# Eight vector-by-matrix units of a modulation moved to VectorE, three operations a step, with their buffer refilled by halves

## The reference

```python
def hybrid_layer(x, ...):
    ...
    h = rms_norm(x, g_ffn_pre)
    gate, up = jnp.split(jnp.matmul(h, w_gate_up), [FFN_HIDDEN], axis=-1)
    f = jnp.matmul(jax.nn.silu(gate) * up, w_down)
    return x + rms_norm(f, g_ffn_post)

# second block
mod_l = jnp.split((jax.nn.silu(c) @ w_ada[i] + b_ada[i])[:, None, :], 6, axis=-1)
mod_c = jnp.split((jax.nn.silu(c_ctx) @ w_ada[i] + b_ada[i])[None, None, :], 6, axis=-1)
hc = modulate(xc, mod_c[0], mod_c[1])
hl = modulate(xl, mod_l[0], mod_l[1])
```

## Time and profile before

| | us |
|---|---|
| median of three runs | 1605.41 |
| the three runs | 1602.16, 1605.41, 1607.61 |
| the profiled execution's own time | 1604.94 |
| its span, first to last instruction | 1603.1 |
| PE busy in the span | 1555.9 |
| feed-forward blocks 2 to 21 of layer 0 | 150.3 to 275 |
| the same of layer 1 | 486.5 to 615 |

### The profile page before, as it was taken

One profiled execution on the slowest core, in us unless ns is written; L12 is line 12 of the kernel. 1 busy time (PEld: TensorE's weight loads), 2 busy tenths in 40 slices (PEclk: granted clock), 3 DMA queues, 4 the chain that ended last, 5 costly groups with the idle time before them and its releaser, 6 DMA issues.

```text
span 1603.1 us, 23911 instructions
## 1 busy us (share of the span) xinstructions
PE 1555.9 (97%) x9646; PEld 1181.9 (74%) x9646; DVE 851.7 (53%) x1388; ACT 612.3 (38%) x1110; POOL 331.6 (21%) x256
## 2 busy tenths in 40 slices
PE   7999999999999999999999999999999999999997
PEld 6888899869888998888787888898644445444442
DVE  5654457456464575579767776346433323333223
ACT  4653444345553444554446665333211111111110
POOL 4440222014321110000036665243300000000000
PEclk9999999999999999999999999999999999999999
DMA  8653997527439986333427666957999999999995
GB/s 281 219 158 116 299 288 229 192 86 265 138 104 268 286 262 238 96 102 105 131 62 221 194 197 203 283 142 282 376 406 424 422 423 425 422 422 424 421 423 211
DMA packets 249971, 410.49 MB, mean 256 GB/s; under 512 B 7685, under 2 KB 196689, under 8 KB 228480
## 3 DMA queue, kind: packets, MB, share of 16 engines
q1 hardware_dynamic: 242864, 379.09, 68.2%
q10 hardware_dynamic: 3584, 19.86, 3.2%
q0 software_dynamic: 3408, 9.95, 1.8%
HBM read 407.72 MB, written 1.15 MB: 255 GB/s over the span
## 4 chain that ended last, share of the span: by engine, by line
PE 86%; DMA 7%; DVE 3%; issue 1%; ACT 1%; POOL 1%; SPq 0%; ACTq 0%; DVEq 0%; POOLq 0%
PE ps L144 84%; PE ps L146 2%; DMA arena<-in_w_expert_gate 2%; DMA arena<-in_w_expert_up 2%; DVE arena L154 1%; DMA ring<-in_w_gate_up 1%; DMA arena<-in_w_ada 1%; DVE arena L150 1%; DMA ring<-in_w_out 1%; ACT split_r L148 1%; POOL split_r L150 1%; DVE split_r L150 0%; DMA rows<-in_b_s 0%; ACT arena L148 0%; POOL arena_r L150 0%
## 5 line engine op out<-in xcount | busy, mean ns | idle before, releaser
L144 PE MATMUL ps<-arena_r,split_r 128*128 128x256 f32 (+1 forms) x2984 | 460.8, 289 | 4.3 <-POOL split_r L150 2.6
L144 PEld LDWEIGHTS ps<-arena_r,split_r 128*128 128x128 f32 x2984 | 394.8, 189 | 21.0 <-issue 15.7
L148 ACT ACTIVATE split_r<-ring 128x1024 fp32r<-128x1024 f32 (+1 forms) x293 | 296.4, 1019 | 257.2 <-PE ps L144 190.1
L150 DVE TENSOR_TENSOR split_r<-ring,split_r 128x1024 fp32r<-128x1024 f32 (+1 forms) x213 | 268.7, 1267 | 205.7 <-ACT split_r L148 205.3
L144 PE MATMUL ps<-split_r,arena_r 128*128 128x512 f32 (+1 forms) x1520 | 340.4, 378 | 7.3 <-issue 3.5
L144 PEld LDWEIGHTS ps<-split_r,arena_r 128*128 128x128 f32 x1520 | 276.3, 189 | 53.2 <-issue 11.3
L144 PE MATMUL ps<-arena 128*64 128x512 f32 (+8 forms) x1232 | 301.5, 469 | 3.5 <-ACT arena L148 1.5
L144 PE MATMUL ps<-hhh_r,split_r 128*128 128x256 f32 (+1 forms) x976 | 228.4, 322 | 0.0
L144 PE MATMUL ps<-ring,arena 128*64 128x512 f32 (+2 forms) x688 | 225.9, 575 | 2.6 <-DMA rows<-in_w_expert_gate 1.0
L150 POOL TENSOR_TENSOR split_r<-ring,split_r 128x1024 fp32r<-128x1024 f32 (+1 forms) x80 | 180.1, 2251 | 215.6 <-ACT split_r L148 187.2
L144 PEld LDWEIGHTS ps<-arena 128*64 128x64 f32 (+2 forms) x1232 | 120.5, 150 | 112.7 <-issue 102.2
(11 more groups left out here) (163 smaller groups left out, 1357.1 us busy)
## 6 DMA issues: line engine op xcount, KB each, us to landing
ring<-in_w_gate_up SPq DMA_DIRECT2D x88, 512.0 KB, 8.1
ring<-in_w_in SPq DMA_DIRECT2D x57, 512.0 KB, 5.4
arena<-in_w_ada SPq DMA_DIRECT2D x24, 1024.0 KB, 7.6
arena<-in_w_expert_gate SPq DMA_DIRECT2D x12, 2048.0 KB, 25.4
ring<-in_w_down SPq DMA_DIRECT2D x22, 1024.0 KB, 4.9
ring<-in_w_expert_up SPq DMA_DIRECT2D x11, 2048.0 KB, 24.9
ring<-in_w_expert_down SPq DMA_DIRECT2D x11, 2048.0 KB, 26.8
ring<-in_w_in SPq DMA_DIRECT2D x28, 768.0 KB, 6.3
```

Of the source, the lines that this page charges most:

```text
L144: made = e.matmul(*a, **k)
L148: made = e.activation(*a, **k)
L150: made = e.tensor_tensor(*a, **k)
```

## The change

Units 6, 7 and 8 leave PE and go to DVE, so that all eight one-vector units (4 to 11) are DVE's. Each is done in three blocks, with three, three and two operations, where it was two in each of four. The units begin at other blocks: in layer 0 at 4, 6, 8, 10, 13, 17, in layer 1 at 4, 7, 10, 13, 16, 19. Unit 11 thus ends in block 21, and its column sum and addition stand after the last block. The last operation of units 6 to 9 writes in fours, as unit 9's did and as the copies of 6 to 8 did.

SyncE loads blocks 4 and 5 ahead of the first unit of a layer. A unit's first half is issued when the fourth operation of the unit before has been made, the second half when the eighth has; one further block of weights goes between the two.

```diff
-        ADA_AT = ({4: 0, 6: 1, 8: 2, 10: 3, 12: 4, 16: 5}, {3: 6, 5: 7, 7: 8, 9: 9, 13: 10, 17: 11})
-        ADA_BY_DVE = (4, 5, 9, 10, 11)
+        ADA_AT = ({4: 0, 6: 1, 8: 2, 10: 3, 13: 4, 17: 5}, {4: 6, 7: 7, 10: 8, 13: 9, 16: 10, 19: 11})
+        ADA_BY_DVE = range(4, 12)
...
+                def ada_closed(m):
+                    for u in ada_ended(l, m):
+                        ada_sums(u)
+                        if u in ADA_BY_DVE:
+                            drop(("am", u))
...
+                    ada_closed(m)
                     for u in ada_begun(l, m):
                         ada_products(u)
+                ada_closed(22)
...
-                for k in range(2 * part, 2 * part + 2):
+                for k in range(3 * part, min(3 * part + 3, 8)):
...
-                        then(v.stt(bk, row(k), cs[:, k, 0:1], bk, ALU.mult, ALU.add))
+                        then(v.stt(bk, row(k), cs[:, k, 0:1], bk, ALU.mult, ALU.add), *([("am", u, "half", 0)] if k == 3 else []))
...
+                for u in ada_ended(l, 22):
+                    modulated_by(u)
...
-                for m, u in ADA_AT[l].items():
+                load_to(up[6])
+                turn = list(ADA_AT[l].items())
+                for x in range(len(turn) + 1):
                     for h in range(2):
-                        modulation(u, h)
-                    load_to(up[m + (5 if u not in ADA_BY_DVE else 8)])
-                    y.wait_ge(*at("am", u))
+                        if x:
+                            m, u = turn[x - 1]
+                            load_to(up[(m + 1 + h if u in ADA_BY_DVE else m) + 5])
+                            y.wait_ge(*at("am", u, "half", h))
+                        if x < len(turn):
+                            modulation(turn[x][1], h)
```

More of the change, by code:

```diff
@@ L537, in program @@
         slot_for = lambda r, k: expert_slots[k % (10 if r == 0 else 8)]
-        ADA_AT = ({4: 0, 6: 1, 8: 2, 10: 3, 12: 4, 16: 5}, {3: 6, 5: 7, 7: 8, 9: 9, 13: 10, 17: 11})
-        ADA_BY_DVE = (4, 5, 9, 10, 11)
+        ADA_AT = ({4: 0, 6: 1, 8: 2, 10: 3, 13: 4, 17: 5}, {4: 6, 7: 7, 10: 8, 13: 9, 16: 10, 19: 11})
+        ADA_BY_DVE = range(4, 12)
         ada_begun = lambda l, m: [u for a, u in ADA_AT[l].items() if u not in ADA_BY_DVE and a == m]
-        ada_step = lambda l, m: [(u, m - a) for a, u in ADA_AT[l].items() if u in ADA_BY_DVE and a <= m < a + 4]
-        ada_ended = lambda l, m: [u for a, u in ADA_AT[l].items() if m == a + (1 if u not in ADA_BY_DVE else 4)]
+        ada_step = lambda l, m: [(u, m - a) for a, u in ADA_AT[l].items() if u in ADA_BY_DVE and a <= m < a + 3]
+        ada_ended = lambda l, m: [u for a, u in ADA_AT[l].items() if m == a + (1 if u not in ADA_BY_DVE else 3)]
         steps = [(c, d) for c in range(16) for d in range(2)]
@@ L883, in ada_products @@
                             made = t.matmul(bk[32 * x:32 * x + 32, :], cs[:, 2 * x + k, :], AW[:, x // 2, 2 * (x % 2) + k, :], k == 0, k == 1)
-                    made.then_inc(*sig(s_mm, ("am", u)))
+                    made.then_inc(*sig(s_mm, ("am", u), ("am", u, "half", 0), ("am", u, "half", 1)))
                 def ada_sums(u):
@@ L2020, in products_kept @@
                     v.wait_ge(*at("ada", u - 2))
[L2021 to L2024, removed]
+                then(v.copy(AD[u % 2], B("am", u)), ("am", u, "kept"))
             def modulation(u, part):
@@ L2046, in modulation @@
                             made = v.stt(o, row(k), cs[:, k, 0:1], bk, ALU.mult, ALU.add)
-                        then(made, ("am", u), ("am", u, "kept"))
+                        then(made, ("am", u), ("am", u, "kept"), ("am", u, "half", 1))
             def modulated_by(u):
```

## The result

The changed kernel takes 1602.32 us in the median (1596.83 to 1606.63), the kernel before on the same chip 1604.36 (1602.16 to 1608.3). The ratio is 0.9982, 95% interval 0.9973 to 0.999: 2.9 us less, within 1.6 and 4.3. The forecast was 1599.3 us, 5.9 less: the time lies inside its range of 1596 to 1603.5, and the gain is half of what was forecast.

What follows compares the result with a forecast made beforehand. The prediction took PE, busy 1555.9 of 1603.1 us, to bound the kernel. Its terms, - 5.58 - 2.75 - 0.3 + 2.75, gave - 5.9 us: 1599.3 us forecast, range 1596 to 1603.5.

Steps and rivals of the forecast that it cites:

- Products removed: Units 6, 7 and 8 lose their eight products on PE, 1.86 us each: 5.58 us gone.
- The wait for unit 7: Layer 1: PE's 2.75 us wait for unit 7's w_ada load goes, if nothing else is late in its place.
- the margin of 0.4 us at block 6: Layer 1: block 6's second quarter split ready at about 512.3, needed at 512.7; cost taken as 0.
- Three operations a step: DVE's 24 more operations in layer 1, up to three a step, fit with 0.5 us spare: cost 0.
- The end of layer 1: Behind block 21, the last sum waits for DVE's last operations: PE idle once, 2.75 us later.
- The start of layer 0: PE's 1.67 us wait before block 4 goes, 1.4 returns at unit 1: 0.3 us gone.
- Halves and order: Loads: refilling units by halves with a block of weights between makes SyncE wait for DVE, at cost 0.
- The sum: Whole kernel: all terms together give 5.9 us less, 1599.1 against the profiled execution, 1599.5 against the median.
- Rival 3: Kernel's end: a DMA-paced stream that doesn't move with PE takes the gain, leaving 1605; chance 0.07.
- rival 2: Layer 1: block 6 or 7 is late and 2.75 us return at a split: - 3.1, 1602.1; chance 0.16.

Runs made afterwards that it cites:

- e1: The changed kernel run again without any edit: 1601.52 us, ratio 0.9982 to the kernel before.
- e11: The changed kernel without the line that loads blocks 4 and 5 ahead of the first unit: 1602.59 us, ratio 0.9986 to the kernel before.
- e9: e7 with units 1 to 5 of layer 0 begun one block later (7, 9, 11, 14, 18): 1591.51 us, ratio 0.9914 to the kernel before.
- e12: The changed kernel run a third time without any edit: 1601.69 us, ratio 0.9979 to the kernel before.
- e8: The kernel before with only blocks 4 and 5 loaded ahead of the first unit of w_ada: 1610.05 us, ratio 1.0032 to the kernel before.
- e7: The changed kernel with layer 1's last sum two steps into the down projection, plus the last pair of gate weights loaded in halves: 1595.92 us, ratio 0.9947.
- e6: The changed kernel with layer 1's last sum behind the first step of the down products: 1599.14 us, ratio 0.996 to the kernel before.
- e3: The changed kernel with layer 1's last sum two steps into the down projection: 1597.37 us, ratio 0.9963 to the kernel before.
- e10: e7 run again without any edit: 1593.11 us, ratio 0.9926 to the kernel before.

## Why the prediction was right, and where it was not

**Products removed, - 5.58.** Right, and a little low: PE's busy time fell by 5.6. From block 2 of layer 1 to the down projection the kernel before took 615.59 - 486.48 = 129.11 us, the changed one 608.64 - 485.71 = 122.93, 6.18 less. The waits are 0.25 of it (2.75 - 2.50), which leaves 5.93 for three units. The 0.35 beyond 5.58 is in the blocks: one directly behind a unit's products or a column sum took 5.85 us or more (517.30 to 523.15 in the earlier trace rows), one behind another block 5.76. The Trainium skill (TensorE: Matmul & The Clock Gate, section Measured speedup vs the span model) gave the estimate of 2.4 us a unit, 7.3 in sum. The trace doesn't agree: 5.93. The down projection's first row before, where after has 608.64:

```profile
615.59 24.68 PE L144 MATMUL ps<-split_r,arena_r 128*128 128x512 f32 x103
```

**The wait for unit 7, - 2.75.** Right, with the margin of 0.4 us at block 6 sufficient: 34.64 us for six blocks without a gap. What was not foreseen is how it varies: this wait read 2.75, 2.09 and 1.84 in three traces of the old layer 1, so its average worth is nearer to 2.2.

**Three operations a step, 0.** Right. In the changed kernel the 48 that write to PSUM take 0.754 to 0.758 us, and DVE is idle 0.62 us ahead of the next gating product even in a step with three.

**The end of layer 1, + 2.75.** The mechanism is right, the direct size a little high: 2.50 in each of four traces. The operations took the 0.76 and 0.75 of the rows; the rest was shorter. PE ended block 21 at 608.08 - 2.50 = 605.58, the gating product ended at 606.45 (0.87 later, not 1.03), and PE started 0.05 us after DVE, not 0.14. The Trainium skill (VectorE: DVE Perf Modes, section on the TRN2 errata) happened to give an estimate of 2.5, but by operations of 0.66 us, and the trace has 0.76 and 0.75. What the step had wrong is that the idle was priced at its length. In e1 and e11 the clock behind it was half for another 1.7 us.

**The start of layer 0, - 0.3.** The step took one reading for a constant. With blocks 4 and 5 ahead, unit 1 was late by 0.58 to 2.87 us in nine traces, 1.85 in the mean and 1.4 forecast; with the unit ahead, block 4 was late by 1.52 to 1.71 in four. So the term is + 0.2 on average, - 1.0 in the profiled execution, and up to + 1.2 with half clock behind it in two of the nine. The range given, - 1.67 to + 0.5, was too narrow above. The argument that the engines' full share leaves no slack fell too: e9 has the wait gone and nothing in its place at a share of 1.03. The bytes were not short; unit 1 was due a block too early. That each term of the DMA stream was worked out to 0.1 us from a single trace was the mistake.

**Halves and order, 0.** Right for the sum: e11 and e12 can't be told apart. The refill by halves has no run of its own. And e8 shows what the order of the loads costs with the old units, 4 to 5 us, since unit 6 is then due behind block 3. With the units changed no harm and no gain can be seen.

**The sum.** 6.9 us at the end of layer 1, with 5.9 forecast, is also what the parts of the profiled execution give (- 5.6 - 2.75 + 2.5 - 1.0), but partly by luck. The changed kernel was 0.34 us ahead at block 2 of layer 0 (150.30 and 149.96), 1.65 behind the last sum of that layer (274.88 and 273.23) and 0.77 at block 2 of layer 1 (486.48 and 485.71): between the layers, in code that the change doesn't touch, it lost 0.9 again (PE stood 1.97 us at 377.62, where it had stood 1.07 at 379.95). Layer 1 gave 6.18, where the terms for it make 5.85. What the forecast left out lies 400 and 950 us later, again in untouched code: 3.0 us gained at the GpSimd split, 3.2 lost at the gate weights. **Rival 3** (a DMA-paced end takes the gain) came true in part, for the reason that the prediction denied, "each load waits for work that shifts too": the issues did shift, but from issue to landing the last gate transfer took longer. Before and after, to landing:

```profile
arena<-in_w_expert_gate SPq DMA_DIRECT2D x1, 2048.0 KB, 37.8
```

```profile
arena<-in_w_expert_gate SPq DMA_DIRECT2D x1, 2048.0 KB, 39.2
```

But the end is not paced by DMA: e7 loads the same bytes in halves, and the wait goes. It was the size of the piece that PE waits for.

**From the profile to the median.** For the profiled execution, 1598.59, the sum of 1599.1 fits, but in the main by luck: it was one of the six quick ones, and the 3.0 us gained and the 3.2 lost behind layer 1, neither of them in the sum, cancel. For the median the forecast was 3 us low: it had twice the gain that was measured, and the time lies in the range because the range reached up to rival 2. By the table, a typical execution of the changed kernel against one of before: products - 5.6, old wait of layer 1 - 2.2, sum + 2.5 and 0.4 x 1.7 of half clock, layer 0 + 0.2 and a fifth of 1.7, GpSimd split - 1.2 and half of 1.7, gate weights + 1.5 and nearly 1.7. That is - 5.6 - 2.2 + 3.2 + 0.5 - 2.1 + 3.1 = - 3.1, where 2.9 was measured. It is an estimate from few traces and shows that no further term is needed, not that each is exact.

**Left open.** Why the GpSimd split waits less, and the last gate transfer takes 1.1 to 1.6 us longer to land (38.9 to 39.3 us in the seven traces that load it whole, 37.7 or 37.8 in those of before), in every kernel with units 6 to 8 on DVE. e8 and e11 place both with the units, not with the order of the loads. How they get there was not tried.

## What to carry to other kernels

An idle of PE is to be priced with what the clock does behind it: if it is near 2 us or longer, add up to 1.7 us, and it pays to put a few independent products ahead of the wait, even if they cover only half of it (e6, e3). A wait that hangs on DMA should be read in several executions before its size goes into a sum. Where PE waits for a transfer in a full stream, first ask whether it can be due one block later or come in halves; the full share of the engines doesn't say that it can't.

## What the runs showed of the hardware

**Half clock follows an idle, not always.** In the fourteen traces of the study, from 12 us on, where the record of the clock begins, PE has 253 idles of 0.4 to 1.72 us, and behind none of them did the granted clock fall from 1.00 to 0.50. Of 68 idles from 1.76 us upward, 49 had it. All 49 stretches ahead of the last microseconds of the program stand behind such an idle; two of them, behind the 1.77 us near 1124 us in e6 and e7, lasted twice as long as the rest. The length alone doesn't decide: 2.50 us at the same instruction was hit in e1 and e11 and not in the first trace nor in e12, while the idle of 2.57 to 2.59 us near 360 us, in code that no run touches, was hit in 13 of 14, and the 1.77 us near 1124 in 12 of 14. What makes the difference was not tried. Each single stretch that was read cost 1.5 to 1.7 us.

**The time of an execution goes with its mean clock.** The changed kernel in e12 took from 1597.07 us at 0.995 to 1608.28 at 0.990. e10 and e9, without an idle of 2 us at the sum or at the gate weights, took 1592.47 to 1594.3 at 0.996 to 0.997 and 1589.14 to 1592.71 at 0.995 to 0.997, six runs each. That fewer long idles also make the times less scattered is not shown: e11 has both idles and spreads over 4.9 us in twelve runs, e7 has neither and spreads over 5.3 in six.

**Landings in a shared stream vary.** The slower half of unit 1, at the same place in the queue, landed 9.9 to 11.6 us after its issue in the nine traces with blocks 4 and 5 ahead of the first unit and unit 1 at block 6. In the three with 10.0 us or less PE stood 0.58 to 1.07 us for it, in the six with 10.7 or more 2.03 to 2.87.
